# Latent attention's head preparation: three stages turned into one, with heads stacked by part and weights regrouped on load

## The chip, the core and the metric

One NeuronCore of a Trainium2 chip runs one launch of the kernel. The metric is the device time of the launch in microseconds. Engines are named as in the profile: PE (TensorE; PEld its weight loads), DVE (VectorE), ACT (ScalarE), POOL (GpSimd) and SP (SyncE, which issues the transfers).

## What is computed

Two transformer blocks over 512 tokens of width 1024. The change touches one part of the first mixer, latent attention ("MLA"), up to its scores. From two normalised latents, `c_q` (256 wide) and `c_kv` (128 wide), and one shared positional part `k_rope` (32 wide), it makes the queries, keys and values of 8 heads:

```python
q = (rms_norm(c_q, cq_norm) @ w_uq).reshape(B, S, H, dn + dr)       # 8 heads, dn=64, dr=32
kv = (rms_norm(c_kv, ckv_norm) @ w_ukv).reshape(B, S, H, dn + dv)   # dv=64
k = jnp.concatenate([kv[..., :dn], jnp.broadcast_to(k_rope[:, :, None, :], (B, S, H, dr))], axis=-1)
v = kv[..., dn:]
q = rms_norm(q, q_norm)      # over the 96 of one head
k = rms_norm(k, k_norm)
q = jnp.concatenate([q[..., :dn], rope(q[..., dn:], pos)], axis=-1)
k = jnp.concatenate([k[..., :dn], rope(k[..., dn:], pos)], axis=-1)
return causal_block_attention(q, k, v).reshape(B, S, H * dv)
```

`rms_norm` divides by the root of the mean square and multiplies by a gain; `rope` turns the two halves of the last 32 features by an angle that depends on the position: `[x1*cos - x2*sin, x1*sin + x2*cos]`. All of it is in float32.

## The kernel before, in words

The program is a row of stages. Each is a block in which every engine has its own list of instructions, tied by semaphores (`stage`, L36), and ends in a barrier of all engines. Within `mixer_even` (L1549) the stages around the change are:

- `ev_in` (input products; its SP list `load_rest`, L1605 to L1624, ends with the loads of `uq` and `ukv`, the weights `w_uq` and `w_ukv`, as they lie in memory), then stages of the other attention's compressed branch.
- `ev_out_load` (L1849): fills, and SP's loads of the tables `cos`, `sin` and `turn` (L1869).
- `ev_nsa` (L1887): the first attention. Beside it SP runs `fill` (L1871 to L1876): two small fills of slots and 27 of zero blocks of 512 KB in DRAM, which a later part needs.
- `ev_mla_in` (`products`, L207, called at L1907): for each head two products for q (96 columns of `uq`, two halves of the contraction, L227) and one for k (64 columns of `ukv`); then four for the values. VectorE copies each result out of PSUM (L241, L1896) and for every head the shared part `kr` into rows 64 to 96 of `km` (L1895). A ring of 8 PSUM banks.
- `ev_mla_norm` (`norm_features`, L247, called at L1908): 16 tiles of 96 rows by 512 (q and k of each head). GpSimd squares (L278), a product with ones sums over the 96 rows into all 96 rows (L306), ScalarE takes Ln and Exp(-0.5 x) in batches of four (L289, L294), VectorE sharpens the reciprocal root by a Newton step in three operations, tiles in pairs (L320, L322, L324), and scales by it and the gain (L336).
- `ev_rope` (L1913): for each tile one 32x32 product that swaps and signs the halves of the positional rows (L1928), and three operations on VectorE, each waiting for the one before (L1936 to L1938). SP waits here until the zero blocks are filled (L1916).
- `ev_mla` (L1946): attention over the heads; its first product is at L383, with `q` and `k` tiles of 96 rows.

Tensors are laid out with the features on the 128 partitions and the 512 tokens along the free axis. A float32 product of 512 columns shows as two weight loads and two matmul records in the trace.

## Time and profile before

| | |
|---|---|
| median of 3 runs | 2620.56 us (2612.14 to 2627.29) |
| profiled execution | 2611.72 us |
| its span in the trace | 2609.8 us |
| mean granted clock of TensorE | 0.887 of full speed |
| busy share of the span | PE 84%, DVE 54%, ACT 38%, POOL 8% |

A row of a window view gives for each engine its busy time and the number of records in that stretch, then the granted clock of TensorE as a share of full speed, the mean busy share of the 16 DMA engines, and the GB/s moved. Times of day are microseconds from the start of the span.

### The profile page before, as it was taken

To read this page: it belongs to the slowest core of one execution; us is meant where nothing else is said; L and a number is where in the kernel's file an instruction comes from. 1 tells how busy PE (TensorE), PEld (TensorE's weight loads), DVE (VectorE), ACT (ScalarE), POOL (GpSimd) and SP (SyncE) were. 2 spreads that over 40 slices of the span, in tenths; PEclk is the share of its full clock that TensorE was granted. 3 is DMA by queue.
4 is the path that set the end of the run, shared out by engine and by line. 5 is a ranking of instruction groups with operands and counts; after the bars stand their busy time and mean duration, and the time that the engine had idled before them with its cause. 6 is when DMAs were issued, how large, how long until landed. Compare 5 with 4: busy or idle time off the path is not lost. (4 is left out here: it accounts for less than half of the span.)

```text
span 2609.8 us, 34405 instructions
## 1 busy us (share of the span) xinstructions
PE 2185.8 (84%) x12786; PEld 1643.6 (63%) x12786; DVE 1403.1 (54%) x2012; ACT 993.4 (38%) x1272; POOL 211.2 (8%) x222
## 2 busy tenths in 40 slices
PE   4957777588999998998799999996798778775995
PEld 3736331146888886877688888885475357455774
DVE  1342767864323324452566666665376766244886
ACT  2121654163322312131456566653253610023775
POOL 0010002000000000000211001111012200001111
PEclk8975897588999998998799999998898879586998
DMA  7100500002313415202677778776311000106996
GB/s 187 56 16 1 220 1 0 32 33 76 118 55 115 124 45 154 72 33 73 199 282 273 273 280 285 277 274 215 102 65 35 1 1 1 64 5 178 377 375 259
DMA packets 212419, 341.49 MB, mean 131 GB/s; under 512 B 40149, under 2 KB 125013, under 8 KB 212318
## 3 DMA queue, kind: packets, MB, share of 16 engines
q1 hardware_dynamic: 203886, 316.94, 35.5%
q0 software_dynamic: 8432, 23.23, 2.5%
q8 instruction: 60, 0.98, 0.2%
q14 instruction: 41, 0.34, 0.0%
HBM read 311.72 MB, written 28.39 MB: 130 GB/s over the span
## 5 line engine op out<-in xcount | busy, mean ns | idle before, releaser
L1388 DVE TENSOR_TENSOR moe_pass_wL<-moe_pass_w,moe_pass_wH 128x2048 fp32r<-128x2048 f32 (+1 forms) x146 | 308.2, 2115 | 153.3 <-ACT moe_pass_wH L1330 153.3
L1330 ACT ACTIVATE moe_pass_wH<-moe_pass_w 128x2048 fp32r<-128x2048 f32 (+1 forms) x146 | 258.5, 1776 | 141.3 <-PE PS L549 110.9
L1388 DVE TENSOR_TENSOR hm_pass_wL<-hm_pass_w,hm_pass_wH 128x2048 fp32r<-128x2048 f32 x62 | 140.1, 2286 | 38.1 <-ACT hm_pass_wH L1330 38.1
L547 PE MATMUL PS<-moe_pass_wL,moe_pass_xgH 128*128 128x512 f32 (+1 forms) x384 | 149.0, 388 | 3.7 <-DVE moe_pass_xgL L1393 3.7
L547 PE MATMUL PS<-xnT_low,ffn_upH 128*128 128x512 f32 x352 | 139.9, 398 | 5.9 <-DVE xnT_low L863 5.6
L549 PE MATMUL PS<-moe_pass_wH,moe_pass_xgH 128*128 128x512 f32 (+1 forms) x384 | 143.6, 374 | 0.0
L548 PE MATMUL PS<-moe_pass_wH,moe_pass_xgL 128*128 128x512 f32 (+1 forms) x384 | 143.6, 374 | 0.0
L549 PE MATMUL PS<-ffn_xH,ffn_upH 128*128 128x512 f32 x352 | 140.3, 399 | 0.0
L548 PE MATMUL PS<-ffn_xH,ffn_up_low 128*128 128x512 f32 x352 | 138.8, 394 | 0.0
L1330 ACT ACTIVATE hm_pass_wH<-hm_pass_w 128x2048 fp32r<-128x2048 f32 x62 | 117.0, 1912 | 19.4 <-DMA hm_pass_w<-in_exp_w_gate 6.4
L870 DVE TENSOR_TENSOR ffn_hT<-ffn_sg,PS 128x512 f32<-128x512 f32 x22 | 15.1, 687 | 169.3 <-PE PS L549 169.3
L289 ACT ACT_TABLE_LOAD x8 | 10.3, 1283 | 243.4 <-PE PS L306 243.3
L1292 PE MATMUL PS<-moe_pass_w,moe_pass_xgO 128*32 128x128 f32 x2816 | 93.7, 274 | 0.0
L1292 PEld LDWEIGHTS PS<-moe_pass_w,moe_pass_xgO 128*32 128x32 f32 x2816 | 80.8, 110 | 13.1 <-issue 13.1
L547 PEld LDWEIGHTS PS<-moe_pass_wL,moe_pass_xgH 128*128 128x128 f32 x384 | 72.7, 189 | 23.9 <-issue 13.0
L830 ACT ACTIVATE ffn_sg<-PS 128x512 f32<-128x512 f32 x22 | 13.2, 599 | 190.4 <-PE PS L549 190.4
L547 PE MATMUL PS<-xnT_low,od_in_wH 128*128 128x512 f32 x192 | 75.6, 394 | 5.8 <-DVE od_W_low L680 5.8
L547 PEld LDWEIGHTS PS<-xnT_low,ffn_upH 128*128 128x128 f32 x352 | 66.6, 189 | 21.4 <-DVE ffn_up_low L848 5.8
L549 PEld LDWEIGHTS PS<-moe_pass_wH,moe_pass_xgH 128*128 128x128 f32 x384 | 72.6, 189 | 10.8
L548 PEld LDWEIGHTS PS<-moe_pass_wH,moe_pass_xgL 128*128 128x128 f32 x384 | 72.7, 189 | 9.2
L547 PE MATMUL PS<-hm_pass_wL,hm_pass_xgH 128*128 128x512 f32 x160 | 65.4, 409 | 14.1 <-DVE hm_pass_wL L1388 8.5
L548 PEld LDWEIGHTS PS<-ffn_xH,ffn_up_low 128*128 128x128 f32 x352 | 66.5, 189 | 16.9
(761 smaller groups left out, 5221.3 us busy)
## 6 DMA issues: line engine op xcount, KB each, us to landing
moe_pass_w<-in_moe_w_down SPq DMA_DIRECT2D x40, 1024.0 KB, 5.0
moe_pass_w<-in_moe_w_gate SPq DMA_DIRECT2D x34, 1024.0 KB, 6.7
moe_pass_w<-in_moe_w_up SPq DMA_DIRECT2D x32, 1024.0 KB, 6.8
hm_pass_w<-in_exp_w_gate SPq DMA_DIRECT2D x44, 512.0 KB, 5.5
hm_pass_w<-in_exp_w_up SPq DMA_DIRECT2D x40, 512.0 KB, 6.0
hm_pass_w<-in_exp_w_down SPq DMA_DIRECT2D x40, 512.0 KB, 5.7
od_W<-in_od_w_in SPq DMA_DIRECT2D x12, 1024.0 KB, 11.3
moe_pass_w<-in_moe_w_gate SPq DMA_DIRECT2D x16, 768.0 KB, 5.1
```

The source lines that it names most:

```text
L289: nc.scalar.activation(rs[rows, g % (2 * B), 0:n], PS[rows, g % 8, 0:n], ACT.Ln, bias=ec[rows, 0:1], scale=1.0 / groups[g]["n"]).then_inc( ...
L547: nc.tensor.matmul(out, lh, rl, start=start, stop=False)
L548: nc.tensor.matmul(out, ll, rh, start=False, stop=False)
L549: return nc.tensor.matmul(out, lh, rh, start=False, stop=stop)
L830: nc.scalar.activation(sg[:, c % 2], PS[:, c % 2, :], ACT.Silu).then_inc(s["silu"], 1)
L870: nc.vector.tensor_tensor(hT[:, c], sg[:, c % 2], PS[:, 2 + c % 2, :], ALU.mult).then_inc(s["hidden"], 1)
L1292: ins = nc.tensor.matmul(over(PS, m, c)[j * OVER:(j + 1) * OVER], xgO[:, k], ring.columns(w, i - 1 + k // HK, R, k % HK)[:, j * P:(j + 1) ...
L1330: nc.scalar.activation(wH[:, i % S, 0:n], w[:, i % R, 0:n], ACT.Copy).then_inc(s["high"], 1)
L1388: nc.vector.tensor_tensor(wL[:, i % S, 0:n], w[:, i % R, 0:n], f32(wH[:, i % S, 0:n]), ALU.subtract) \
```

## The change

One stage, `ev_latent_heads`, takes the place of `ev_mla_in`, `ev_mla_norm` and `ev_rope`. Heads are stacked by part: the 64 non-positional features of two heads fill 128 rows, the 32 positional features of the four even heads (and of the four odd ones) fill 128 rows, and so do the same features with their halves swapped. For this the weights are loaded in regrouped columns, and `ukv` as all keys and then all values. The sums of squares of all heads go to 8 rows of one bank, through products with a 0/1 matrix `pick`; the root is taken once on those 8 rows for q and once for k, and products with a matrix `spread` (8 rows) lay it out over the stacked rows. The turn is a sum of two VectorE products, with gains laid out by row and the sign in the sine table; the shared part of k is laid out over 128 rows, plain and swapped, by two products with `turn`. The positional rows are then moved into the heads' tiles by 16 transfers from SBUF to SBUF. An odd head keeps its positional part in rows 0 to 32, zeros in 32 to 64 and the rest in 64 to 128, so its scores contract over 128 rows. The weights and tables are loaded by `fill`, ahead of the zero blocks, and no longer in `ev_in` and `ev_out_load`. `power` takes Ln and Exp on ScalarE, `square` and `keep_k` square and copy out of PSUM there, `take_v` copies the values. The gains come as one tensor of 128x6, laid out on the host.

```diff
+def rope_spread():
+    turn = np.zeros((ROT, 2, P), np.float32)
+    for m in range(P):
+        turn[m % ROT, 0, m] = 1.0
+        turn[(m + ROT // 2) % ROT, 1, m] = 1.0
+    return turn.reshape(ROT, 2 * P)
+def head_of_row():
+    pick = np.zeros((P, 6, NH), np.float32)
+    for p in range(P):
+        for m in range(4):
+            pick[p, m, 2 * m + p // HD] = 1.0
+        for e in range(2):
+            pick[p, 4 + e, 2 * (p // ROT) + e] = 1.0
+    return pick
...
-                    sp.dma_start(uq[:, :, :], D["mla_w_uq"][0].rearrange("(k p) n -> p k n", p=P)).then_inc(loaded["mla"], 16)
-                    sp.dma_start(ukv[:, :], D["mla_w_ukv"][0]).then_inc(loaded["mla"], 16)
...
-                for dst, src in ((cosT[64:96, :], D["rope_table"][0]), (sinT[64:96, :], D["rope_table"][1]),
-                                 (turn[64:96, :], D["rope_turn"])):
-                    sp.dma_start(dst, src).then_inc(loaded["rope"], 16)
-
         def fill(sp):
+            for dst, src in ((cosT[:, :], D["rope_table"][0]), (sinT[:, :], D["rope_table"][1]),
+                             (turn[64:96], D["rope_spread"].rearrange("p (a n) -> p a n", a=2)),
+                             (pick[:, :, :], D["head_pick"].rearrange("p (a n) -> p a n", a=6)),
+                             (spread[:, :, :], D["head_spread"].rearrange("p (a n) -> p a n", a=6))):
+                sp.dma_start(dst, src).then_inc(loaded["rope"], 16)
+            half = ROT // 2
+            for k in range(2):
+                src = D["mla_w_uq"][0, k * P:(k + 1) * P].rearrange("p (j e c) -> p e j c", e=2, c=MQK)
+                sp.dma_start(uq[:, k, 0:SEQ].rearrange("p (h d) -> p h d", d=HD),
+                             D["mla_w_uq"][0, k * P:(k + 1) * P].rearrange("p (h c) -> p h c", c=MQK)[:, :, 0:HD]).then_inc(loaded["mla"], 16)
+                for e in range(2):
+                    rope, turned = (uq[:, k, a + e * P:a + (e + 1) * P].rearrange("p (j d) -> p j d", d=ROT) for a in (SEQ, SEQ + 2 * P))
+                    sp.dma_start(rope, src[:, e, :, HD:MQK]).then_inc(loaded["mla"], 16)
+                    sp.dma_start(turned[:, :, 0:half], src[:, e, :, HD + half:MQK]).then_inc(loaded["mla"], 16)
+                    sp.dma_start(turned[:, :, half:ROT], src[:, e, :, HD:HD + half]).then_inc(loaded["mla"], 16)
+            for i in range(2):
+                sp.dma_start(ukv[:, i * SEQ:(i + 1) * SEQ].rearrange("p (h d) -> p h d", d=HD),
+                             D["mla_w_ukv"][0].rearrange("p (h c) -> p h c", c=P)[:, :, i * HD:(i + 1) * HD]).then_inc(loaded["mla"], 16)
             for slots in C.slots.values():
...
+            km, vm = sb("km", [P, NH, SEQ], m3), sb("vm", [P, NT, 512], m3)
+            filled = 16 * sum(1 + rows.shape[0] // P for rows in C.made_rows.values())
+            latent_heads(nc, C, cq, ckv, kr, uq, ukv, gm, cosT, sinT, turn, pick, spread, xnT, km, vm, loaded, filled)
...
+                used = slice(0, MQK if h % 2 == 0 else P)
+                jobs.append(dict(q=xnT[used, h], k=km[used, h], v=lambda kb, h=h: vm[:, kb, h * HD:(h + 1) * HD],
...
+def latent_heads(nc, C, cq, ckv, kr, uq, ukv, gm, cosT, sinT, turn, pick, spread, qm, km, vm, loaded, filled):
...
+            step = Steps(pool, s["zeroed"])
+            step(nc.gpsimd.memset(ec[:, :], EPS))
+            for t in (qm, km):
+                step(nc.gpsimd.memset(t[ROT:HD].rearrange("p (j e) n -> p j e n", e=2)[:, :, 1], 0.0))
+        @block.sync
+        def _(sp):
+            for t, out, done in ((qm, qo, s["q_roped"]), (km, ko, s["k_roped"])):
+                for e in range(2):
+                    rows = slice(HD, MQK) if e == 0 else slice(0, ROT)
+                    sp.wait_ge(done, e + 1)
+                    for j in range(4):
+                        sp.dma_start(t[rows, 2 * j + e], out[ROT * j:ROT * (j + 1), e]).then_inc(s["moved"], 16)
+            sp.wait_ge(s["moved"], 16 * 16)
+            sp.wait_ge(loaded["zero"], filled)
+        @block.tensor
+        def _(pe):
+            made = [0]
+            def bank():
+                made[0] += 1
+                return PS[:, (made[0] - 1) % 8, :]
+            def q_nope(m):
+                ps = bank()
+                for k in range(2):
+                    ins = nc.tensor.matmul(ps, uq[:, k, m * P:(m + 1) * P], cq[:, k], start=k == 0, stop=k == 1)
+                ins.then_inc(s["made"], 1)
...
+            def k_rope(i):
+                nc.tensor.matmul(bank(), turn[HD:MQK, i], kr[HD:MQK, :], start=True, stop=True).then_inc(s["made"], 1)
+            def value(t):
+                nc.tensor.matmul(bank(), ckv[:, t * P:(t + 1) * P], ukv[:, SEQ:2 * SEQ], start=True, stop=True).then_inc(s["made"], 1)
+            def spread_out(i, w):
+                nc.tensor.matmul(bank(), spread[:, w], rs[:, i], start=True, stop=True).then_inc(s["made"], 1)
+            pe.wait_ge(loaded["mla"], 16 * 16)
+            pe.wait_ge(loaded["rope"], 80)
+            for m in range(4):
+                q_nope(m)
+            for e in range(2):
+                q_rope(4 + e)
+            k_nope(0)
+            k_nope(1)
+            pe.wait_ge(s["squared"], 6)
+            pe.wait_ge(s["q_copied"], 1)
+            sums = bank()[0:NH]
+            for w in range(6):
+                ins = nc.tensor.matmul(sums, pick[:, w], sq[:, w], start=w == 0, stop=w == 5)
+            ins.then_inc(s["made"], 1)
+            for i in range(2):
+                pe.wait_ge(s["q_copied"], 2 + i)
+                k_rope(i)
+            pe.wait_ge(s["q_copied"], 4)
+            k_nope(2)
+            pe.wait_ge(s["q_cos"], 1)
+            k_nope(3)
+            pe.wait_ge(s["q_cos"], 2)
+            q_rope(6)
+            pe.wait_ge(s["k_copied"], 1)
+            q_rope(7)
+            pe.wait_ge(s["k_copied"], 2)
+            pe.wait_ge(s["squared"], 11)
+            sums = bank()[0:NH]
+            for m in range(4):
+                nc.tensor.matmul(sums, pick[:, m], sq[:, 6 + m], start=m == 0, stop=False)
+            nc.tensor.matmul(sums, C.ones[0:ROT, 0:NH], sq[0:ROT, 10], start=False, stop=True).then_inc(s["made"], 1)
+            pe.wait_ge(s["q_rstd"], 1)
+            spread_out(0, 4)
+            pe.wait_ge(s["k_cos"], 1)
+            spread_out(0, 5)
+            for m, (sem, value_) in enumerate(((s["k_sin"], 1), (s["k_copied"], 3), (s["k_copied"], 4), (s["q_sin"], 1))):
+                pe.wait_ge(sem, value_)
+                spread_out(0, m)
+            pe.wait_ge(s["q_sin"], 2)
+            value(0)
+            pe.wait_ge(s["k_rstd"], 1)
+            pe.wait_ge(s["q_roped"], 1)
+            spread_out(1, 4)
+            spread_out(1, 5)
+            pe.wait_ge(s["q_roped"], 2)
+            spread_out(1, 0)
+            for m in range(1, 4):
+                pe.wait_ge(s["q_done"], 2 * m)
+                spread_out(1, m)
+            pe.wait_ge(s["q_done"], 8)
+            value(1)
+            pe.wait_ge(s["v_taken"], 1)
+            value(2)
+            pe.wait_ge(s["k_roped"], 1)
+            value(3)
...
+            def power(n, i):
+                act.wait_ge(s["made"], n + 1)
+                nc.scalar.activation(rs[:, i], PS[0:NH, n % 8, :], ACT.Ln, bias=ec[0:NH, 0:1], scale=1.0 / N).then_inc(s["logged"], 1)
+                act.wait_ge(s["logged"], i + 1)
+                nc.scalar.activation(rs[:, i], rs[:, i], ACT.Exp, scale=-0.5).then_inc(s["exped"], 1)
...
+            act.wait_ge(s["zeroed"], 1)
+            for m in range(4):
+                act.wait_ge(s["q_copied"], m + 1)
+                nc.scalar.activation(sq[:, m], qr[:, m], ACT.Square).then_inc(s["squared"], 1)
+            for n in (4, 5):
+                square(n, n)
+            for m in range(2):
+                square(6 + m, 6 + m)
+                keep_k(6 + m, m)
+            power(8, 0)
+            square(9, 10, slice(0, ROT))
+            for m in (2, 3):
+                square(9 + m, 6 + m)
+                keep_k(9 + m, m)
+            power(15, 1)
+            for n, t in ((22, 0), (29, 1), (30, 2), (31, 3)):
+                take_v(n, t)
...
+        @block.vector
+        def _(dve):
+            step = Steps(dve, s["steps"])
+            def newton(n, i, done):
+                dve.wait_ge(s["exped"], i + 1)
+                y, t = rs[:, i], tt[:, i]
+                step(nc.vector.scalar_tensor_tensor(out=t, in0=PS[0:NH, n % 8, :], scalar=N * EPS, in1=y, op0=ALU.add, op1=ALU.mult))
+                step(nc.vector.scalar_tensor_tensor(out=t, in0=t, scalar=-0.5 / N, in1=y, op0=ALU.mult, op1=ALU.mult))
+                nc.vector.scalar_tensor_tensor(out=y, in0=t, scalar=1.5, in1=y, op0=ALU.add, op1=ALU.mult).then_inc(done, 1)
+            def gained(dst, src, col, other_):
+                return nc.vector.scalar_tensor_tensor(out=dst, in0=src, scalar=gm[:, col:col + 1], in1=other_, op0=ALU.mult, op1=ALU.mult)
+            def nope(n, i, m, src, dst, done):
+                dve.wait_ge(s["made"], n + 1)
+                for a in range(2):
+                    rows = slice(a * HD, (a + 1) * HD)
+                    nc.vector.scalar_tensor_tensor(out=dst[rows, 2 * m + a], in0=src[rows, m], scalar=gm[rows, 3 * i:3 * i + 1],
+                                                   in1=PS[rows, n % 8, :], op0=ALU.mult, op1=ALU.mult).then_inc(done, 1)
+            for m in range(4):
+                dve.wait_ge(s["made"], m + 1)
+                nc.vector.tensor_copy(qr[:, m], PS[:, m, :]).then_inc(s["q_copied"], 1)
+            for e in range(2):
+                dve.wait_ge(s["squared"], 5 + e)
+                gained(qa[:, e], PS[:, 4 + e, :], 1, cosT[:, :]).then_inc(s["q_cos"], 1)
+            newton(8, 0, s["q_rstd"])
+            dve.wait_ge(s["squared"], 9)
+            gained(ka[:, :], PS[:, 1, :], 4, cosT[:, :]).then_inc(s["k_cos"], 1)
+            dve.wait_ge(s["made"], 11)
+            gained(kb[:, :], PS[:, 2, :], 5, sinT[:, :]).then_inc(s["k_sin"], 1)
+            dve.wait_ge(s["k_cos"], 1)
+            dve.wait_ge(s["k_sin"], 1)
+            nc.vector.tensor_tensor(ka[:, :], ka[:, :], kb[:, :], ALU.add).then_inc(s["k_turned"], 1)
+            for e in range(2):
+                dve.wait_ge(s["made"], 14 + e)
+                gained(qb[:, e], PS[:, 5 + e, :], 2, sinT[:, :]).then_inc(s["q_sin"], 1)
+            dve.wait_ge(s["q_cos"], 2)
+            dve.wait_ge(s["q_sin"], 2)
+            nc.vector.tensor_tensor(qa[:, :, :], qa[:, :, :], qb[:, :, :], ALU.add).then_inc(s["q_turned"], 1)
+            dve.wait_ge(s["q_turned"], 1)
+            for e in range(2):
+                dve.wait_ge(s["made"], 17 + e)
+                nc.vector.tensor_tensor(qo[:, e], qa[:, e], PS[:, e, :], ALU.mult).then_inc(s["q_roped"], 1)
+            newton(15, 1, s["k_rstd"])
+            for m in range(4):
+                nope(18 + m, 0, m, qr, qm, s["q_done"])
+            dve.wait_ge(s["k_turned"], 1)
+            for e in range(2):
+                dve.wait_ge(s["made"], 24 + e)
+                nc.vector.tensor_tensor(ko[:, e], ka[:, :], PS[:, (23 + e) % 8, :], ALU.mult).then_inc(s["k_roped"], 1)
+            for m in range(4):
+                nope(25 + m, 1, m, kn, km, s["k_done"])
```

## Rows read from the trace of the kernel before

**Rows 1.** Busy time of each engine in three stretches, one per old stage (window view).

```profile
386.00:413.50 27.50, 26.64 (x56) 7.53 (x56) 16.38 (x28) 0.00 (x0) 0.00 (x0) 1.00 0.00 1
413.50:473.00 59.50, 23.85 (x33) 5.79 (x32) 48.73 (x66) 29.41 (x40) 18.53 (x17) 0.63 0.00 0
473.00:511.00 38.00, 27.48 (x32) 5.34 (x32) 33.14 (x48) 0.00 (x0) 0.00 (x0) 0.50 0.00 0
```

**Rows 2.** Timeline of the input stage: start, us, engine, line, operation.

```profile
386.86 1.93 PE L227 MATMUL PS<-ev_latent,ev_uq 128*96 128x512 f32 x4 [1.55 <-PEq L42]
...
410.49 0.19 PEld L227 LDWEIGHTS PS<-ev_ukv,ev_latent 128*128 128x128 f32 x1 [0.24 <-issue]
...
410.92 0.19 PEld L227 LDWEIGHTS PS<-ev_ukv,ev_latent 128*128 128x128 f32 x1 [0.24 <-issue]
```

**Rows 3.** Timeline of the turning stage and the start of the attention behind it.

```profile
476.10 0.17 PEld L1928 LDWEIGHTS PS<-xnT,ev_turn 32*32 32x32 f32 x1 [0.68 <-issue]
...
476.96 0.17 PEld L1928 LDWEIGHTS PS<-xnT,ev_turn 32*32 32x32 f32 x1 [0.68 <-issue]
...
509.64 0.69 DVE L1938 TENSOR_TENSOR ev_km<-ev_km,PS 32x512 f32<-32x512 f32 x1
...
511.62 0.77 PE L383 MATMUL PS<-ev_km,xnT 96*128 96x128 f32 x2 [10.57 <-PEq L42]
```

**Rows 4.** Groups by line in the norm stage: busy us, mean ns | idle before.

```profile
L324 DVE SCALAR_TENSOR_TENSOR ev_mla_norm_rs<-ev_mla_norm_tt,ev_mla_norm_rs 96x512 f32<-96x512 f32 x16 | 13.3, 871 | 0.3
L322 DVE SCALAR_TENSOR_TENSOR ev_mla_norm_tt<-ev_mla_norm_tt,ev_mla_norm_rs 96x512 f32<-96x512 f32 x16 | 13.1, 859 | 0.3
L289 ACT ACTIVATE ev_mla_norm_rs<-PS,ev_mla_norm_eps 96x512 f32<-96x512 f32 x16 | 10.4, 681 | 11.1 <-PE PS L306 11.1
L320 DVE SCALAR_TENSOR_TENSOR ev_mla_norm_tt<-PS,ev_mla_norm_rs 96x512 f32<-96x512 f32 x16 | 10.3, 682 | 9.4 <-ACT ev_mla_norm_rs L294 9.1
L294 ACT ACTIVATE ev_mla_norm_rs<-ev_mla_norm_rs 96x512 f32<-96x512 f32 x16 | 8.8, 617 | 0.0
```

**Rows 5.** Timeline of the norm stage.

```profile
421.55 1.28 ACT L294 ACT_TABLE_LOAD   x1
...
422.85 2.19 ACT L294 ACTIVATE ev_mla_norm_rs<-ev_mla_norm_rs 96x512 f32<-96x512 f32 x4
...
430.16 0.75 DVE L336 SCALAR_TENSOR_TENSOR xnT<-xnT,ev_gmq,ev_mla_norm_rs 96x512 f32<-96x512 f32 x1
...
430.82 0.74 DVE L336 SCALAR_TENSOR_TENSOR ev_km<-ev_km,ev_gmk,ev_mla_norm_rs 96x512 f32<-96x512 f32 x1
```

**Rows 6.** Group of a GpSimd fill ahead of the first attention.

```profile
L1852 POOL MEMSET xnT<- 64x2048 f32 x1 | 1.8, 1800 | 38.0 <-POOLq L42 38.0
```

**Rows 7.** SP's issues by line: ns min/median/max, first and last start; landing in us.

```profile
L1600 SPq DMA_DIRECT2D ev_W<-in_ev_w_in x16: 507/508/2785, 18.3 to 33.9; - x16
...
L2238 SPq DMA_DIRECT2D s_fox<-s_decay x4: 577/590/622, 1906.1 to 1908.1; - x4
...
DMA to landing us min/median/max: 6.2/6.7/7.4
...
DMA to landing us min/median/max: 1.7/1.7/2.0
...
L1876 SPq DMA_DIRECT2D hm_pass_made<-ev_zero x8: 1175/1188/1200, 292.9 to 301.5; - x8
```

The first landing line belongs to L2238, the second to L2241, which issues the same small transfer (one row of 512 floats from SBUF to SBUF) 85 us later. Each transfer of L1600 moves 512 runs of 256 bytes.

**Rows 8.** Windows inside other stretches: 32x32, 128x8 and 32x128 tiles, then attention with and without DMA.

```profile
489.00:495.00 6.00, 6.00 (x9) 1.23 (x8) 5.72 (x9) 0.00 (x0) 0.00 (x0) 0.50 0.00 0
1872.00:1874.00 2.00, 2.00 (x6) 0.44 (x5) 0.00 (x0) 0.00 (x0) 0.00 (x0) 1.00 0.96 318
2012.00:2013.00 1.00, 1.00 (x6) 0.44 (x4) 0.00 (x0) 0.26 (x2) 0.00 (x0) 0.50 1.06 317
290.00:310.00 20.00, 17.42 (x87) 8.62 (x85) 15.51 (x55) 14.07 (x42) 0.00 (x0) 1.00 0.84 342
330.00:350.00 20.00, 17.29 (x87) 8.62 (x87) 14.38 (x48) 12.70 (x38) 0.00 (x0) 1.00 0.00 1
```

More of the change, by code:

```diff
@@ L1541, in rope_tables, with gains_by_row @@
     ang = np.arange(SEQ, dtype=np.float32)[None, :] * inv[:, None]
-    turn = np.zeros((ROT, ROT), np.float32)
-    for m in range(half):
-        turn[m + half, m] = -1.0
-        turn[m, m + half] = 1.0
-    return np.stack([np.tile(np.cos(ang), (2, 1)), np.tile(np.sin(ang), (2, 1))]).astype(np.float32), turn
+    cos, sin = np.cos(ang), np.sin(ang)
+    return np.stack([np.tile(cos, (8, 1)), np.tile(np.concatenate([-sin, sin]), (4, 1))]).astype(np.float32)
+def rope_spread():
[12 more added lines that the diff above has]
+    return pick
+def gains_by_row(q, k):
+    out = np.zeros((P, 6), np.float32)
+    for i, g in enumerate((q, k)):
+        rope = g[HD:MQK]
+        out[:, 3 * i] = np.tile(g[:HD], 2)
+        out[:, 3 * i + 1] = np.tile(rope, 4)
+        out[:, 3 * i + 2] = np.tile(np.roll(rope, ROT // 2), 4)
+    return out
 def mixer_even(nc, C, D, x, xnT):
@@ L1608, in load_rest @@
                               (gckv[:, :], column(D["mla_ckv_norm"][0])),
[L1609 to L1610 removed]
+                              (gm[:, :], D["mla_gains"])]
                     for a in (0, HD):
@@ L1905, in mixer_even @@
-            for t in range(NT):
-                jobs.append(([(ckv[:, t * P:(t + 1) * P], vcols)], slice(0, P), slice(0, SEQ), copy_to(nc, vm[:, t])))
-            products(nc, C, "ev_mla_in", jobs, lambda n: [(loaded["mla"], 32)] if n == 0 else [])
-            norm_features(nc, C, "ev_mla_norm", [
-                dict(src=[t[0:MQK, h]], gain=[g[0:MQK, 0:1]], dst=[t[0:MQK, h]], ones=C.ones[0:MQK, 0:MQK], n=MQK)
-                for h in range(NH) for t, g in ((qm, gmq), (km, gmk))])
-            with stage(nc, "ev_rope", "turned steps") as (block, s):
-                @block.sync
-                def _(sp):
-                    sp.wait_ge(loaded["zero"], 16 * sum(1 + rows.shape[0] // P for rows in C.made_rows.values()))
-                r = slice(64, 96)
-                tiles = [t[r, h] for h in range(NH) for t in (qm, km)]
-                PS = C.PS
-                @block.tensor
-                def _(pe):
-                    pe.wait_ge(loaded["rope"], 48)
-                    for n, tile in enumerate(tiles):
-                        if n >= 8:
-                            pe.wait_ge(s["steps"], 3 * (n - 7))
-                        nc.tensor.matmul(PS[r, n % 8, :], turn[r, :], tile, start=True, stop=True).then_inc(s["turned"], 1)
-                @block.vector
-                def _(dve):
-                    step = Steps(dve, s["steps"])
-                    dve.wait_ge(loaded["rope"], 48)
-                    for n, tile in enumerate(tiles):
-                        dve.wait_ge(s["turned"], n + 1)
-                        step(nc.vector.tensor_tensor(tile, tile, cosT[r, :], ALU.mult))
-                        step(nc.vector.tensor_tensor(PS[r, n % 8, :], PS[r, n % 8, :], sinT[r, :], ALU.mult))
-                        step(nc.vector.tensor_tensor(tile, tile, PS[r, n % 8, :], ALU.add))
```

65 lines of the change are left out of this document (40 added, 25 removed).

## The prediction

> **What bounds it now.** Stages are fenced by barriers, so the page's busy shares over the whole span say nothing of one stage; I read first the busy time of each engine stage by stage [rows 1], then the order of time at the edges. From the first product of the old stages (386.86 us, [rows 2]) to the first score product of latent attention (511.62, [rows 3]) there are **124.8 us**, in three stages. In the first TensorE is the bound (26.64 of 27.5 us, granted clock 1.00, that is 2.4 GHz). In the second no engine is full; VectorE has 48.7 of 59.5 us. In the third VectorE has 33.1 of 38 us, and TensorE runs at 0.50 (1.2 GHz). The attention stages before and after stay, so what the three stages lose the kernel loses: all that follows is moved up.
>
> The groups by line [rows 4] give prices. In the norm stage VectorE does three Newton steps and one scaling for each of 16 tiles (8 heads of q and k); in the turning stage three operations a tile, each waiting for the one before.
>
> **The change, part by part.** Three stages become one. VectorE: 16x3 Newton steps (13.3+13.1+10.3 = 36.7 us) become 2x3; 16 scalings stay, on 64 rows; 48 turning operations become 12 (five for q, three for k, four multiplications by the root); 24 head copies become 4 (those of k go to ScalarE). GpSimd's 16 squares go to ScalarE, whose table loads fall from 8 to 4.
>
> **TensorE.** Before: 28 input products, 16 sums, 16 turns = 60 of 512 columns. After: 8 (q without position) + 4 (q positional) + 4 (k) + 6 (sums of q's squares) + 2 (the shared k part) + 4 (q turned) + 5 (sums of k's squares) + 12 (spreading the roots) + 4 (values) = **49**. Each is an f32 product and has two records. In the value products they start 0.43 us apart [rows 2], 0.856 us a product at 1.00; in the turning stage 0.86 us apart [rows 3], 1.71 us a product at 0.50 (also: 32 rows cost what 128 do, so the 128 rows that odd heads now score over instead of 96 cost nothing). Where tile shapes alternated, 28 products took 26.64 us, 0.95 each: I take 0.856 and 0.12 us for each of seven changes of shape, with 0.95 throughout (4 us more) as the upper bound.
>
> I walk the written order at full clock from the first product. 14 input products: 12.0. VectorE copies q, ScalarE squares at 0.68 (as the Ln of such a tile, [rows 4]); the last square of q is done at 11.2, no stall. Six sums: 17.4. Then the root of q: 0.25 until the sum is seen, table load 1.28, Ln 0.68, load 1.28, Exp 0.62, three chained Newton steps at 0.73 (0.68 [rows 4] and a wait): 6.3, ready at 23.7. Beneath it TensorE has eight products and five sums, to 28.9: hidden (it would cost 6.3 uncovered). The root of k, 6.2 more: 35.1. Above it TensorE has six spreads and one value product, to 35.1: just covered, and each us more in that chain lengthens the stage by one. From here **VectorE sets the end**: 8 products of q at 0.67 (430.16 to 430.82, [rows 5]) to 40.4, two of k's positional part to 41.8, 8 of k to **47.1**. TensorE's last spreads and three values end beside it, at 43.0.
>
> SyncE moves 16 blocks of 32 rows into place. Eight lie beside q's products. The last eight start at 41.1 and take 0.59 us each to issue and 1.7 to land [rows 7]: 47.5. On a crowded queue landing took 6.7 (same rows): 52.5; here nothing else moves data, so 47.5. The zeroing on GpSimd (two of 32 rows by 2048; 1.8 us for such a fill on 64 rows, [rows 6]) lies under the 12 us of the first products, and nobody waits for it; uncovered 3.6. Last operation to first score: 511.62-510.33 = 1.3 [rows 3]. Sum at full clock: **48.9 against 124.8, a saving of 75.9**; at 0.95 a product 72.
>
> A table load starts at 421.55 and its Exp at 422.85 [rows 5], 1.30 a switch. The Trainium skill, "ScalarE: Activation LUTs", section "What ACT_TABLE_LOAD costs", adds about 1.38 us of draining to each switch; by that k's chain would be 2.8 us longer and the stage with it. The row shows no such drain, and I go by the row.
>
> **The clock** is the disputed term. On 32x32 tiles TensorE was busy without a gap over 489 to 495 and stayed at 0.50 [rows 8], as in the whole stage [rows 1]. On 128x8 tiles, coming from full ones, it held 1.00 [rows 8]; the new sums are 128x8, so they should hold it. The new spreads have 8 rows and 128 columns; the nearest is a 32x128 product, at 0.50 in its stretch [rows 8]. So they lie between two rows, nearer to the low one. Of the 16 products after the sums of k, 12 are spreads. If the clock is low for none of them, the stage ends as above; for all 16, TensorE ends at 55.6 and the last value copy at 56.6, 9.1 more; I take the fall after the first four: 52.2 and 53.2, **5.7 more**. The next stage starts at 0.50 now [rows 1] and, after 5 us without TensorE work or from a low clock, will again: no gain there.
>
> **What moves elsewhere.** Two weight loads leave the input stage; 16 regrouped ones and 5 tables go to the head of the queue that SyncE issues under the first attention (270 to 386). Their runs of 256, 128 and 64 bytes: 2x(1024+1024+2048) + 2x1024 = 10,240. Nearest row: 16 DMAs of 512 runs of 256 bytes were issued from 18.3 to 34.4 [rows 7]; with 6.7 to land that is 22.8 us for 8192, 2.8 ns a run; here 29 us, from 271 to 300, 86 us early. Queued behind them are 2 slot fills and 27 zero blocks, issued until 302.7 now (301.5+1.2, [rows 7]), then until about 332; they are awaited only at the new stage's end, near 435. Nothing; uncovered each us would count. The attention beside the DMAs loses nothing to them: 87 matmuls in 290 to 310 at DMA 0.84, 87 in 330 to 350 at none [rows 8]; at most 1 us.
>
> **Rivals.**
> - **A, the clock holds:** saving 75.9. For: 128x8 held it. Against: 32x32 never won it.
> - **B, it falls in the spreads:** saving 75.9-5.7 = 70.2. My forecast.
> - **C, it is low from the first sums on:** 12.0 + 35x1.71 + 1.0 + 1.0 (last copy) + 1.3 = 75.2, saving 49.6; in the whole stage 49x1.71+3.3 = 87, saving 37.7. Against: the 128x8 stretch.
> - **D, the pipeline does not form** as the edit says: both root chains exposed, 43.0+6.3+6.2+12 (VectorE's tail)+1.3 = 68.8, saving 56.0. Against: q's chain has 5 us of cover.
> - **E, slower: the regrouped loads come late.** Place: the new stage's first wait, at 386.9. It costs from there on, and the kernel is slower than before once they land after 386.9+70 = 457, 186 us for 10,240 runs, 18 ns a run, six times the row. The 256-byte runs moved 2.1 MB in 22.8 us, 92 GB/s, against 342 GB/s of whole rows in 290 to 310 [rows 8]: a loss of nearly four times that 86 us of slack swallow. The Trainium skill, "DMA: Bandwidth & Descriptors", section "Specifications", gives 512 bytes as the least for line rate, with a read-modify-write below; by that rule this is where the change could fail, and the trace agrees with the loss though not with one that reaches the path.
>
> **Numbers.** The profiled execution took 2611.72 us (span 2609.8 and 1.9 around it); the median, 2620.56, is 8.84 above. B: 2611.72-70.2 = 2541.5, against the median **2550.4**. A: 2544.7. D: 2564.6. C: 2571.0 to 2582.9. The three times lie up to 8.4 from their median, so the low end is 2544.7-8 = 2537; the high end 2571 takes in D and the mild C. Chances: A 0.34, B 0.42, C 0.13, D 0.07, E 0.03, and 0.01 for no gain for another reason. A to D gain over 0.5% (13 us, what a measurement of this kernel can tell from no change): faster 0.96; E and the rest are split, same 0.02, slower 0.02.
>
> **Right or wrong.** In the new profile: first product to first score near 54.6 us (B) or 49 (A). The spreads at 1.71 or 0.86 us a product and the granted clock of their stretch. TensorE's wait for k's roots under 1 us. VectorE busy near 27 us, ScalarE near 20. The last moves landing within 3 us of VectorE's end. No wait for weights at the start; the zero blocks issued by 332. I am wrong if the clock is 0.50 before the spreads, if ScalarE loads a table for Square or Copy, or if the first product waits for a DMA.

## The result, and the profile after

| | kernel before | changed kernel |
|---|---|---|
| median, same chip, side by side | 2620.18 us | 2538.82 us (2534.28 to 2543.81, 4 runs) |
| ratio | | 0.9691, 95% interval 0.9657 to 0.9724 |
| profiled execution, its span | 2611.72, 2609.8 us | 2534.28, 2531.6 us |
| first product of the heads to first score | 124.76 us | 56.97 us |
| the attention behind it | 57.33 us | 54.68 us |
| output product behind that | 51.21 us | 51.85 us |
| all that follows | 1989.6 us | 1981.2 us |

The change makes the kernel 3.1% faster: 81.4 us by the medians, where 70.2 were forecast. The lower rows show which microseconds are its own. The two profiled spans differ by 78.2 us. The stage gives 67.8 and the attention 2.7, together 70.4; the output product takes 0.6 more. The other 8.4 lie in later code that the change does not touch; repeated (below) that part took 1989.4 us, as before. In the other twelve profiles of this document, all of which share that code, it takes 1983.6 to 1993.4 us, and the 1981.2 here are the shortest. So these 8.4 are scatter between executions.

The stage after, in one window (busy us and records per engine, granted clock, DMA share, GB/s), against the three of [rows 1]:

```profile
386.90:443.90 57.00, 55.51 (x99) 19.14 (x99) 27.51 (x38) 18.33 (x27) 3.56 (x2) 0.79 0.08 19
```

VectorE falls from 98 us of work to 27.5, ScalarE from 29 to 18; TensorE is busy for 55.5 of 57 us, so it is the bound. Its timeline (start, length, operation, tile rows*columns, records, two a product):

```profile
386.91 7.11 PE L1993 MATMUL PS<-ev_latent,ev_uq 128*128 128x512 f32 x16 [1.71 <-PEq L42]
...
397.28 1.88 PE L2003 MATMUL PS<-ev_latent,ev_ukv 128*128 128x512 f32 x4
399.09 5.32 PE L2027 MATMUL PS<-lh_sq,ev_pick 128*8 128x512 f32 x12
404.34 1.98 PE L2006 MATMUL PS<-ev_latent,ev_turn 32*128 32x512 f32 x4
...
411.60 3.60 PE L2046 MATMUL PS<-lh_sq,ev_pick 128*8 128x512 f32 x8
415.13 1.02 PE L2047 MATMUL PS<-lh_sq,ones 32*8 32x512 f32 x2
416.08 8.79 PE L2012 MATMUL PS<-lh_rs,ev_spread 8*128 8x512 f32 x12
424.80 2.08 PE L2009 MATMUL PS<-ev_ukv,ev_latent 128*128 128x512 f32 x2
426.80 10.60 PE L2012 MATMUL PS<-lh_rs,ev_spread 8*128 8x512 f32 x12
437.34 5.07 PE L2009 MATMUL PS<-ev_ukv,ev_latent 128*128 128x512 f32 x6
443.88 2.62 PE L383 MATMUL PS<-ev_km,xnT 96*128 96x128 f32 x10 [1.48 <-PEq L42]
```

No row of TensorE within the stage carries a wait: the pipeline forms. Sums of squares run at 0.89 us a product, the second six spreads at 1.77. Windows of the same kernel show when the clock goes and comes back:

```profile
416.00:418.00 2.00, 2.00 (x6) 0.95 (x6) 0.69 (x1) 1.80 (x2) 0.00 (x0) 0.99 0.00 0
418.00:437.00 19.00, 19.00 (x23) 6.50 (x21) 14.21 (x20) 1.39 (x3) 0.00 (x0) 0.50 0.23 55
441.00:443.00 2.00, 1.40 (x3) 0.25 (x1) 0.00 (x0) 1.16 (x2) 0.00 (x0) 0.79 0.00 0
443.00:444.00 1.00, 0.12 (x1) 0.14 (x2) 0.00 (x0) 0.04 (x1) 0.00 (x0) 1.00 0.00 0
```

Full clock (2.4 GHz) up to 418, some two spreads after they begin, then 0.50 (1.2 GHz) with TensorE busy without a gap; in the last of three full-size value products it rises, and the attention starts at 1.00, where it started at 0.50 before. ScalarE's timeline around the roots, then rows of VectorE's, then SyncE's issues of the loads, the zero blocks and the last eight moves:

```profile
400.42 1.28 ACT L2085 ACT_TABLE_LOAD   x1
404.45 0.68 ACT L2085 ACTIVATE lh_rs<-PS,lh_ec 8x512 f32<-8x512 f32 x1 [2.74 <-PE PS L2027]
405.14 1.28 ACT L2087 ACT_TABLE_LOAD   x1
406.44 0.63 ACT L2087 ACTIVATE lh_rs<-lh_rs 8x512 f32<-8x512 f32 x1
...
416.18 0.68 ACT L2085 ACTIVATE lh_rs<-PS,lh_ec 8x512 f32<-8x512 f32 x1 [5.41 <-PE PS L2047]
416.88 1.28 ACT L2087 ACT_TABLE_LOAD   x1
```

```profile
420.26 0.68 DVE L2120 SCALAR_TENSOR_TENSOR lh_rs<-lh_tt,lh_rs 8x512 f32<-8x512 f32 x1
...
430.62 0.69 DVE L2162 TENSOR_TENSOR lh_ko<-lh_ka,PS 128x512 f32<-128x512 f32 x1 [0.95 <-PE PS L2012]
...
437.45 1.53 DVE L2129 SCALAR_TENSOR_TENSOR ev_km<-lh_kn,ev_gm,PS 64x512 f32<-64x512 f32 x2 [0.18 <-PE PS L2012]
```

```profile
273.12 0.60 SPq L1899 DMA_DIRECT2D ev_uq<-in_mla_w_uq  x1
...
282.59 1.34 SPq L1907 DMA_DIRECT2D ev_ukv<-in_mla_w_ukv  x2
...
308.23 9.87 SPq L1913 DMA_DIRECT2D hm_pass_made<-ev_zero  x8
...
429.70 4.95 SPq L1978 DMA_DIRECT2D ev_km<-lh_ko  x8
```

The table for Ln is loaded while ScalarE still waits for the sum (it ends at 401.70, the sum comes at 404.45), so each chain of roots holds one load, not two. The last rows of VectorE wait for TensorE's spreads. The zero blocks are all issued by 318.1, where [rows 7] have 302.7. The regrouped loads are issued from 273.1 to 283.9 and land a median 2.5 to 4.1 us later by their size.

### The profile page after: what moved, and what is told of

Same layout as the page of the kernel before. It is cut to its first block and busy times, and to the rows that moved or that the text cites. A ratio compares the mean times of both kernels' runs of the same rounds, so it can differ in the third digit from the quotient of the medians.

```text
span 2531.6 us, 34168 instructions
## 1 busy us (share of the span) xinstructions
PE 2150.8 (85%) x12764; PEld 1636.9 (65%) x12764; DVE 1329.5 (53%) x1910; ACT 982.4 (39%) x1259; POOL 194.2 (8%) x208
## 5 line engine op out<-in xcount | busy, mean ns | idle before, releaser
L547 PEld LDWEIGHTS PS<-moe_pass_wL,moe_pass_xgH 128*128 128x128 f32 x384 | 72.4, 188 | 23.6 <-issue 12.7
L549 PEld LDWEIGHTS PS<-ffn_xH,ffn_upH 128*128 128x128 f32 x352 | 66.4, 189 | 16.3
## 6 DMA issues: line engine op xcount, KB each, us to landing
od_W<-in_od_w_in SPq DMA_DIRECT2D x12, 1024.0 KB, 10.8
```

The lines of the kernel that those rows point to most:

```text
L547: nc.tensor.matmul(out, lh, rl, start=start, stop=False)
L549: return nc.tensor.matmul(out, lh, rh, start=False, stop=stop)
```

## The experiments

**The changed kernel again**, as the base of the first group.

> The changed kernel once more, to separate what the change does from how two profiled executions differ. In its profile so far the new stage takes 57.0 us (first product to first score) against 124.8 before, the attention behind it is 2.7 us shorter, and 7.7 us of the 78.2 us gained in the span lie in later stages that the edit does not touch. Theory 1 (executions differ): new stage 57 +-0.5, attention behind it 54.7 +-0.5, and the stretch from there to the end comes out different from the first profile by some us, of either sign; ratio 0.967 to 0.973. Rival (the edit speeds up later stages, by another layout of memory for one): the same 7 to 8 us reappear in the same later stages, ratio 0.966 to 0.970.

Measured: 2542.54 us, ratio 0.9741 (0.9726 to 0.9755) to 2608.7 us. Stage 55.28 us, attention 54.40, the rest 1989.4. The stage is 1.7 us shorter than in the first profile, more than the 0.5 allowed for by the theory, and the 7 to 8 us in later stages that the rival wanted did not come back. The six first spreads took 7.74 us, against 8.79 in the profile above; window rows of this kernel:

```profile
418.00:420.00 2.00, 2.00 (x6) 0.85 (x5) 0.35 (x1) 1.46 (x2) 0.00 (x0) 1.00 0.00 0
420.00:422.00 2.00, 2.00 (x5) 0.86 (x4) 1.81 (x4) 1.13 (x2) 0.00 (x0) 0.84 0.14 33
422.00:424.00 2.00, 2.00 (x3) 0.69 (x3) 1.93 (x4) 0.00 (x0) 0.00 (x0) 0.50 0.42 98
```

The spreads begin at 418.42 and the clock falls at some 421.4, after three to four of them. So the point of the fall moves between executions by a product or two, and with it the stage.

**Spreads on more rows.** The 8 rows of roots and of `spread` are laid into tiles of more rows, the others zeros: the sums, the results and the number of products stay. The diff for 64 rows (128 and 32 rows likewise):

```diff
-        pick, spread = sb("pick", [P, 6, NH]), sb("spread", [NH, 6, P])
+        pick, spread = sb("pick", [P, 6, NH]), sb("spread", [64, 6, P])
...
-        rs, tt, ec = sb("rs", [NH, 2, SEQ]), ...
+        rs, tt, ec = sb("rs", [64, 2, SEQ]), ...
...
+            step(nc.gpsimd.memset(rs[:, :, :], 0.0))
...
-             "head_spread": lambda: head_of_row().transpose(2, 1, 0).reshape(NH, 6 * P),
+             "head_spread": lambda: np.pad(head_of_row().transpose(2, 1, 0).reshape(NH, 6 * P), ((0, 64 - NH), (0, 0))),
```

The lines left out keep Ln, Exp and the Newton steps on the first 8 rows, and let ScalarE wait for the fill of `rs`.

> The 12 products that lay out the roots contract over 128 rows (8 of data, 120 of zeros) instead of 8. In the changed kernel the clock went from 1.00 to 0.50 some 2 us after the first of them and the rest ran at 1.71 us a product. Theory 1 (the clock falls because the tiles have few rows): it stays at 1.00, the 12 products take 0.86 us each, TensorE's part ends 9 to 10 us sooner, and VectorE's last products and the last moves set the end: the stage takes 48 to 50 us, 7 to 9 us less, ratio to the kernel before 0.965 to 0.967. Theory 2 (it falls for another reason, such as the waits between the products): it falls at the same place, the stage stays at 57 us, the time is that of the changed kernel.

> As the 128-row form, but over 64 rows (8 of data, 56 of zeros). If the clock follows the rows of the tile, this may go either way; if it holds, the stage takes 48 to 50 us as with 128 rows, if it falls 57 us as with 8. If it falls with 128 rows as well, rows have nothing to do with it.

> The version with 64-row spreads once more, as the base of the next three. The stage again 48.7 us (48.65 in the earlier run), against 55.3 and 57.0 of the changed kernel with its 8-row spreads; the whole kernel 0.971 of the kernel before.

> The spreads on 32 rows (24 of them zeros). If 32 rows behave as 8 do, as the 32x32 and 32x128 products of the kernel before did, the clock falls among the spreads: 1.71 us a product and a stage of 55 to 57 us. If they behave as 64 rows do: 0.86 us, clock 1.00, 48.7 us. Between them: the clock falls later than with 8 rows, 50 to 54 us.

| rows of a spread | six first spreads | stage | attention | whole kernel | ratio to before |
|---|---|---|---|---|---|
| 8 (changed kernel) | 8.79, 7.74 us | 56.97, 55.28 | 54.68, 54.40 | 2538.82, 2542.54 | 0.9691, 0.9741 |
| 32 | 8.03 us | 56.64 | 56.08 | 2544.33 | 0.9724 (0.9678 to 0.977) |
| 64 | 5.41 us | 48.65, 48.64 | 54.59, 54.59 | 2534.36, 2534.82 | 0.9712 (0.9682 to 0.9742), 0.9689 (0.9643 to 0.9735) |
| 128 | 5.42 us | 48.66 | 56.72 | 2533.96 | 0.9704 (0.9684 to 0.9725) |

Of the 64-row kernel (second run), its timeline and windows; then one window of the 32-row kernel:

```profile
417.33 5.41 PE L2013 MATMUL PS<-lh_rs,ev_spread 64*128 64x512 f32 x12
...
429.05 4.94 SPq L1979 DMA_DIRECT2D ev_km<-lh_ko  x8
...
429.07 2.84 PE L2010 MATMUL PS<-ev_ukv,ev_latent 128*128 128x512 f32 x6
436.80 2.01 PE L383 MATMUL PS<-ev_km,xnT 96*128 96x128 f32 x5 [4.88 <-PEq L42]
```

```profile
417.00:432.00 15.00, 14.91 (x33) 5.68 (x32) 12.86 (x19) 4.43 (x7) 0.00 (x0) 1.00 0.20 48
432.00:436.00 4.00, 0.00 (x0) 0.00 (x0) 3.61 (x5) 0.55 (x1) 0.00 (x0) 1.00 0.35 82
436.00:440.00 4.00, 3.20 (x7) 2.03 (x8) 1.87 (x7) 1.31 (x5) 0.00 (x0) 0.63 0.50 182
```

```profile
420.00:440.00 20.00, 20.00 (x23) 6.82 (x22) 14.92 (x21) 1.09 (x2) 0.00 (x0) 0.50 0.22 53
```

This settles the clock: the same products, equally dense, stay at 1.00 on 64 or 128 rows (four profiles, with that of the late values below) and fall to 0.50 on 8 or 32 (four, with that of the loads in the stage). With 64 rows the stage is 6.6 to 8.3 us shorter, and the path changes hands: TensorE ends at 431.9, and VectorE (435.7) and the last transfers (issued by 433.99, 2.0 us to land) set the end. That is the full-clock walk of the prediction, 48.9 against 48.64 us. In the first group, run side by side, the 64- and 128-row kernels are 8.2 and 8.6 us faster than the changed one by the medians, though single runs of the 64-row kernel overlap with it (2528.28 to 2545.25 us against 2540.56 to 2544.33). By the medians both beat the changed kernel, and with it the kernel before. The whole-kernel gain of 0.965 to 0.967 that was expected of 128 rows was not reached, since its base, the repeat, stands at 0.9741. The 128-row kernel also loses some 2 us again in the attention (56.72 us): there 5.49 us pass without TensorE work, and the first ten records run in 5.04 us, at 0.50.

The Trainium skill, "TensorE: Matmul & The Clock Gate", section "Why this matters for your kernels", says that one product on 32 rows takes as long as on 128. At a given clock this trace agrees: two 32-row products with `turn` take 1.98 us, as two of 128 rows beside them do; spreads at 1.00 take 0.90 us on 64 and on 128 rows, and at 0.50 they take 1.77 on 8, 32 and 64. But over the stage the narrow tile costs 6.6 to 8.3 us, by the clock that it loses.

**Both chains of roots uncovered.** TensorE waits for q's root ahead of the products behind q's sums, and for k's root ahead of the first spread.

```diff
+            pe.wait_ge(s["q_rstd"], 1)
             for i in range(2):
                 pe.wait_ge(s["q_copied"], 2 + i)
                 k_rope(i)
...
-            pe.wait_ge(s["q_rstd"], 1)
+            pe.wait_ge(s["k_rstd"], 1)
             spread_out(0, 4)
...
+            newton(15, 1, s["k_rstd"])
             for e in range(2):
                 dve.wait_ge(s["made"], 17 + e)
                 nc.vector.tensor_tensor(qo[:, e], ...)
-            newton(15, 1, s["k_rstd"])
```

> TensorE waits for the root of q right behind the sums of q's squares, and for the root of k right behind those of k; VectorE takes k's root ahead of q's positional products. All work is the same; only the cover is gone. Theory 1 (the hand-written order hides the two chains): q's chain is exposed by about 5 us (Ln, table load, Exp, three Newton steps; the load ahead of Ln is done before the sum comes), k's by about 5 us, and part of it is given back because the clock then is low for other products or not: 6 to 12 us more than the changed kernel, ratio 0.971 to 0.974. Rival (the chains would not have been seen anyway, TensorE's work at the low clock is the bound in the tail): under 3 us more.

> Both chains of roots exposed again (the same edit as in the exposed version), now with 64-row spreads. There the stage grew by 17 to 18.5 us, of which TensorE's two waits were 4.85 and 4.92. Theory 1: the rest was the clock of the 8-row spreads and of what follows a gap; with 64 rows the products after each gap run at 0.86 us, and the stage grows by 10 to 12 us, to 59 to 61. Theory 2: a gap of 5 us lowers the clock whatever the tiles are, for as long afterwards as before: growth 16 us or more, to 65 or above.

With 8-row spreads: stage 73.83 us, kernel 2558.38, ratio 0.9805 (0.9786 to 0.9824). With 64-row spreads: stage 71.81, kernel 2556.86, ratio 0.9773 (0.9727 to 0.982). The timeline of the second, and its windows:

```profile
411.17 3.77 PE L2007 MATMUL PS<-ev_latent,ev_turn 32*128 32x512 f32 x4 [4.85 <-DVE lh_rs L2122]
414.88 3.32 PE L2004 MATMUL PS<-ev_latent,ev_ukv 128*128 128x512 f32 x4
418.04 3.60 PE L2000 MATMUL PS<-ev_latent,ev_uq 128*128 128x512 f32 x8
...
431.04 10.60 PE L2013 MATMUL PS<-lh_rs,ev_spread 64*128 64x512 f32 x12 [4.92 <-DVE lh_rs L2122]
```

```profile
411.00:415.00 4.00, 3.83 (x5) 1.28 (x5) 0.88 (x3) 0.59 (x1) 0.00 (x0) 0.50 0.00 0
418.00:425.00 7.00, 7.00 (x17) 1.97 (x15) 2.72 (x3) 2.44 (x4) 0.00 (x0) 1.00 0.00 0
431.00:459.00 28.00, 27.96 (x32) 10.01 (x32) 14.69 (x20) 1.79 (x3) 0.00 (x0) 0.51 0.16 38
```

The first expectation (6 to 12 us more) was too low: the stage grew by 16.9 to 18.6 us. Theory 2 of the second holds. The two waits are 4.85 and 4.92 us, 9.8 together, but the 64-row stage grew by 23.2. The rest is clock. After the first gap four products took 6.9 us instead of 3.7. After the second, twelve spreads and four values took 28.1 us instead of 14.6, and the idle 4.9 us at the end shrank to 1.5: 9.8+3.1+13.5-3.4 = 23.0. After the first gap two full-size products brought the clock back; after the second, 64-row spreads did not win back in 28 us what they had kept in the version without the gap. So what the cover of the two chains is worth here is 17 to 23 us of the stage (15.8 and 22.0 us of the kernel by the medians), and only 9.8 of it is waiting.

**The values late.** On the 64-row kernel, the last three value products wait for 2, 4 and 7 of k's 8 multiplications, to keep TensorE working up to the attention.

```diff
             pe.wait_ge(s["q_done"], 8)
+            pe.wait_ge(s["k_done"], 2)
             value(1)
             pe.wait_ge(s["v_taken"], 1)
+            pe.wait_ge(s["k_done"], 4)
             value(2)
             pe.wait_ge(s["k_roped"], 1)
+            pe.wait_ge(s["k_done"], 7)
             value(3)
```

> On the 64-row version, the last three value products wait for VectorE's multiplications of k (2, 4 and 7 of 8), so that TensorE has work until about 1 us before VectorE ends, not some 5 us less. If it is TensorE's idle time before the attention that sometimes costs the clock there, the attention starts at 1.00 and takes 54.6 us or less each time (56.7 with the 128-row spreads, where it started at 0.50), and the stage stays within 0.5 us of 48.7. Rival: three products of 0.86 us with gaps of 0.6 us between them do not hold it, or the start matters less: attention 54.6 to 57 as before. The last value copy on ScalarE now comes late: if it ends after the last transfer, the stage grows by up to 1 us. Whole kernel: within 2 us of the base either way.

```profile
430.42 5.93 PE L2010 MATMUL PS<-ev_ukv,ev_latent 128*128 128x512 f32 x6 [2.06 <-DVE ev_km L2133]
437.83 2.86 PE L383 MATMUL PS<-ev_km,xnT 96*128 96x128 f32 x8 [1.48 <-PEq L42]
```

A miss: the first wait opens a gap of 2.06 us, the clock is down behind it, the three values take 5.93 us instead of 2.84 and become the path. The length of the gap alone does not explain it: in the next experiment 3.04 us pass behind seven full-size products and the clock stays up, while here 64-row spreads stand ahead of the gap. Which of the two mattered was not tested apart. Stage 50.45, attention 54.97, kernel 2537.2 (0.971, 0.9658 to 0.9762): nothing gained.

**The start of the attention.** In the kernel before, seven full-size products (of the identity and a value tile, into a bank that is free by then) follow the last turn, once VectorE has done 9 of the 16 tiles.

```diff
+                    pe.wait_ge(s["steps"], 3 * 9)
+                    for n in range(7):
+                        nc.tensor.matmul(PS[:, 0, :], C.ident[:, :], vm[:, 0], start=True, stop=True)
```

> The kernel before, with seven products of 128x128 tiles added at the end of the turning stage, beside VectorE's last operations, into a bank that is free. They compute nothing. In the changed kernel the attention behind the new stage takes 54.7 us instead of 57.4 and starts at clock 1.00 instead of 0.50. Theory 1 (the attention is shorter because it finds the clock up, after three full products of values): the clock rises to 1.00 before the attention starts, which takes 54.5 to 55 us, and the turning stage stays within 1 us of 38: 1.5 to 2.7 us less in all, ratio 0.999 to 1.000, seen in the profile only. Rival (it is shorter by the new tiles of 128 rows, or by the layout): the attention stays at 57.4 us with the clock up.

The attention's first products and two windows of this kernel: the whole attention, and a stretch within it.

```profile
514.48 2.62 PE L383 MATMUL PS<-ev_km,xnT 96*128 96x128 f32 x10 [3.04 <-PEq L42]
```

```profile
514.48:570.70 56.22, 45.90 (x208) 22.92 (x208) 35.13 (x116) 38.05 (x112) 0.00 (x0) 0.94 0.11 38
540.50:548.50 8.00, 7.60 (x22) 2.93 (x22) 2.82 (x11) 2.95 (x11) 0.00 (x0) 0.57 0.00 1
```

The window of the whole attention in the kernel before, and in the changed one:

```profile
511.62:568.95 57.33, 47.50 (x208) 24.41 (x208) 35.44 (x116) 38.13 (x112) 0.00 (x0) 0.89 0.10 38
```

```profile
443.88:498.56 54.68, 44.40 (x208) 22.41 (x208) 35.08 (x116) 38.05 (x112) 0.00 (x0) 0.97 0.11 39
```

Ratio 1.0003 (0.9985 to 1.002). The first ten records run in 2.62 us, as in the changed kernel, instead of 5.04, yet the attention is only 1.1 us shorter, short of the 54.5 to 55 us expected, and the stage ahead of it is 0.9 longer. A dip of the clock in its middle (the second window) took much of it back. The mean clock over the attention goes 0.89, 0.94, 0.97 and its time 57.33, 56.22, 54.68. The versions that share the changed kernel's tiles line up in nearly the same way: 56.72 us at 0.91 (128 rows), 56.08 and 56.09 at 0.94 (32 rows; chains uncovered), 54.97 at 0.94 (the values late), 54.40 to 54.71 at 0.97. Where two versions start at 1.00 and have 0.94 in the mean, old tiles take 56.22 and new ones 56.1. So the 2.7 us are clock, and not the new tiles. The first ten records account for 2.4 of them, but dips further on differ from version to version: the 64-row kernel starts at 0.63 and takes 54.59, while the two at 56.1 start at full clock. What places the dips stays open, and that the changed kernel has only short ones, late in the attention, in both its profiles is in part luck.

**The regrouped loads in the stage.** The 16 loads stand at the head of the new stage's SyncE list instead of in `fill`, with nothing to hide them.

```diff
         def fill(sp):
...
-            half = ROT // 2
-            for k in range(2):
-                ...
         @block.sync
         def _(sp):
+            half = ROT // 2
+            for k in range(2):
+                ...
```

> The changed kernel with its 16 regrouped weight loads issued at the start of the new stage instead of 115 us ahead, so that their whole cost lies open. Theory 1 (as the issues in the changed kernel's profile show, 0.63 us each for 16 and 4 us to land): the first product waits 11 issue + 4 landing = 14 to 15 us, so the stage takes 71 to 72 us. My prediction's estimate was 2.8 ns a run, 29 us: stage 86 us. Either way far from the 70 us at which the change would have paid nothing, so the loads' rival was never near.

```profile
386.92 0.60 SPq L1963 DMA_DIRECT2D ev_uq<-in_mla_w_uq  x1
...
396.40 1.34 SPq L1971 DMA_DIRECT2D ev_ukv<-in_mla_w_ukv  x2
...
401.07 4.10 PE L1993 MATMUL PS<-ev_latent,ev_uq 128*128 128x512 f32 x5 [15.66 <-DMA ev_ukv<-in_mla_w_ukv]
```

2556.08 us, ratio 0.9789 (0.9761 to 0.9816), against 0.9741 of the changed kernel. From the first issue to the first product 14.15 us, 10.8 of them issuing: 1.4 ns a run, half of the 2.8 estimated. With the 57.0 us from the first product on, the stage takes 71.15, as expected. Behind the wait of 15.66 us the first eight products take 8.82 us instead of 7.11, since the first of them run at the low clock, so the open cost is some 16 us. That is what `fill` hides.

**The Newton steps alone.** The kernel before without its 48 sharpening operations: the reciprocal roots are used as Ln and Exp give them.

```diff
-                for k in range(3):
+                for k in range(3 if sharpen else 0):
...
+                if not sharpen:
+                    dve.wait_ge(s["rstd"], gs[-1] + 1)
```

> The kernel before without the three Newton operations per tile in latent attention's norm stage; the reciprocal roots are used as Exp leaves them. It prices the part of the change that takes the root once per head. Theory 1 (the norm stage is bound by VectorE's chain of Newton steps): the stage falls from 59.5 us to between 25 and 32, where GpSimd's 16 squares (18.5 us) and ScalarE's Ln and Exp with 8 table loads (29.4 us) bound it: 27 to 34 us less, ratio 0.987 to 0.990. Rival (the waits among TensorE, ScalarE and GpSimd through the ring of four squares bind it): under 15 us less.

2593.76 us, ratio 0.9934 (0.9911 to 0.9957). The norm stage is 23.9 us shorter (the turning stage's first product moves from 473.57 to 449.65). Groups by line of what is left in it:

```profile
L306 PE MATMUL PS<-ev_mla_norm_sq,ones 96*96 96x512 f32 x32 | 19.9, 728 | 6.1 <-POOL ev_mla_norm_sq L278 4.4 <-DVE xnT L338 1.6
L278 POOL TENSOR_TENSOR ev_mla_norm_sq<-xnT 96x512 f32<-96x512 f32 x8 | 9.4, 1174 | 0.6
L338 DVE SCALAR_TENSOR_TENSOR ev_km<-ev_km,ev_gmk,ev_mla_norm_rs 96x512 f32<-96x512 f32 x8 | 8.3, 1034 | 0.0
```

36.7 us of VectorE work give 23.9 us of time, less than the 27 to 34 of the theory and more than the 15 of the rival; the whole kernel gains 18.5 us by the medians, and the profiled run is the fastest of its five. Then ScalarE is the fullest (28.8 of 32.5 us in the window from 417), TensorE waits for GpSimd's squares, and the scalings take 1.0 us instead of 0.75 beside them. So the Newton steps alone are about a third of the 70 us. The rest goes with the other engines' per-head work and with one stage in place of three; how it splits between these was not measured.

## Why the prediction was right

**The size.** 70.2 us forecast for the stage; 67.8 and 69.5 measured in two profiles of the changed kernel, 70.5 and 72.4 with the attention. The forecast of 2550.4 lies 11.6 above the median. That is the base of the sum more than the saving: it started from 2620.56, and the kernel before had medians of 2608.70, 2612.28 and 2613.89 in the three later sets of runs, from which the same saving gives 2538.5 to 2543.7. Beside the first of these sets the ratio was 0.9741, which is 67.6 us of 2608.7. So the 81.4 us of the first comparison flatter the change, and the forecast saving lies between the two.

**The walk at full clock** was right to a few tenths, as the 64-row kernel shows with the clock taken out: 48.9 against 48.64. Part of that is luck: k's root is there 1.1 us earlier than the walk had it (34.0), and the tail of VectorE behind it takes 13.5 us where 12.0 were counted, because a multiplication by the root takes 0.77 us and not 0.67. In the changed kernel the sums of k end 29.2 us after the first product (28.9), q's root is ready at 22.3 (23.7), k's at 34.0 (35.1); VectorE has 27.5 us of work (27), ScalarE 18.3 (20), the last transfers take 4.95 us to issue and 2.0 to land (4.7 and 1.7). The term that was off is the chain: 6.3 us with two table loads; 1.28 of them are hidden in front of the Ln, and from the end of the sum to the root 4.8 are measured (404.41 to 409.20). The Trainium skill, "ScalarE: Activation LUTs", section "What ACT_TABLE_LOAD costs", adds a drain of about 1.38 us to each switch; the Ln at 416.18 is followed by the load at 416.88 and the Exp at 418.17, so no drain shows, and going by the row was right.

**The clock, case B.** It held through the 128x8 sums and fell in the spreads, after some two products in one profile and three to four in the other, where four were taken. Each product that moves from high to low clock adds 0.86: two of them make the 54.6 into 56.3, one makes it 55.5. Measured 56.97 and 55.28. Two more errors lie in this sum and nearly cancel. The walk at low clock counts the 33 products up to the sums of k at 0.856 us, 28.2, where the walk at full clock has 28.9 with the changes of shape; with that and spreads at 1.77 instead of 1.71 us TensorE ends later (55.5 us after its first product in the first profile, where 52.2 and the two products make 53.9). Behind it 1.5 us pass to the first score, where 2.3 were counted.

That the spreads lose the clock was inferred from rows which do not show it: the 32x128 products of [rows 8] follow 4.57 us without TensorE work, and the 32x32 ones start low, so these rows show that narrow tiles do not win the clock, and not that they lose it. The four products before the fall had no row at all. Here the guess came true, and the 64-row kernel shows that rows decide it. Rivals A (holds) and C (low from the sums on) fall by the same windows. Rival A's time is real, however: it needs the 64 rows.

**What was wrong.** "No gain there" for the attention failed: the low clock ends in the last of three full-size value products, and TensorE then idles only 1.48 us. It was worth 2.7 us here, though that share depends on dips of the clock further on (56.1 us in two versions that started as well). In the 64-row kernel with its 4.88 us of idle time the clock did fall behind it, as foreseen (0.63 in 436 to 440), and the attention still took 54.59.

**Rival D** stayed away; TensorE never waited. Its price was undersized, though: both chains uncovered and a tail behind them were put at 19.9 us above the walk at full clock, and cost 23.2, of which the clock is the largest part, and no tail of VectorE alone.

**Rival E** was priced twice too dear (29 us for the loads, 14 measured when alone), and the zero blocks were issued by 318, not 332. It was hidden either way. Its reading of 92 GB/s as a loss of nearly four times is wrong: those 16 transfers shared the queue with other loads, and the DMA view of the kernel before has 6.83 MB moved from 18 to 41 us, 297 GB/s in the mean, with 8,512 of 12,394 packets under 512 bytes.

## What to carry to other kernels

Fuse stages when each is short of work on another engine; then walk the merged order by hand at both clock levels, for the bound may move between TensorE's clock and the tail of VectorE and transfers. A product with few rows is as long as a full one but may lose the clock for the whole stretch: where the stage is bound by TensorE, laying the operands into more rows, with zeros, cost nothing that shows here and took 6.6 to 8.3 us from the stage. Price a wait of TensorE not by its length alone: gaps of 2.06, 4.85 and 4.92 us cost 3.1, 3.1 and 13.5 us more in the products behind them, and one of 3.04 us cost nothing.
